# A dense f32r product on TensorE: operand addresses on multiples of 2048 bytes, and moving columns read and written backwards

## The reference: what is computed

```python
# first layer
p = rmsnorm(x, g) @ w_in                    # 1024 x 3076: r, k, v, decay, gates, q, kv, index
y = concat([y_rwkv, y_attn]) @ w_out        # 1024 x 1024
x = rmsnorm(x + y, final_g)
# second layer, mixer: 1024 x 9216, memory of 256 tokens: 1024 x 2048
proj = rmsnorm(x) @ w_in_2
k, vm = split(rmsnorm(mem) @ w_kv_2)
y_a = (gb * conv3(gc * v)) @ w_a_out        # 1024 x 1024
y_b = silu(layernorm(conv31(u * sigmoid(ug)))) @ w_b_out
y_c = attention(q, k, vm) @ w_att_out
x = x + (g0 * y_a + g1 * y_b + g2 * y_c) @ w_o
# second layer, feed-forward: 1024 x 5632, 2816 x 1024
gt, up = split(conv3(rmsnorm(x) @ w_up))
x = x + (silu(gt) * up) @ w_down
out = rmsnorm(x, norm_final_g)
```

## Time and profile before

| | |
|---|---|
| median of 3 runs | 1462.99 us |
| lowest, highest | 1462.32, 1467.27 us |
| span of the profiled execution | 1458.8 us |
| PE busy | 1410.6 us (97%), 7612 matmul records |
| PE weight loads busy | 1142.5 us (78%) |
| VectorE busy | 928.9 us (64%) |
| ScalarE busy | 495.1 us (34%) |
| GpSimdE busy | 493.1 us (34%) |
| mean granted TensorE clock | 0.983 of full speed |

### The profile page before, as it was taken

The page is one execution under the profiler, slowest core; times in us unless marked ns, Lnnn a source line. Parts: engine busy times, 40 slices in busy tenths (PEclk is TensorE's granted clock), DMA queues, the critical chain, the costliest instruction groups (busy, mean ns, idle before and its releaser), DMA issues.

```text
span 1458.8 us, 18647 instructions
## 1 busy us (share of the span) xinstructions
PE 1410.6 (97%) x7612; PEld 1142.5 (78%) x7612; DVE 928.9 (64%) x1327; ACT 495.1 (34%) x679; POOL 493.1 (34%) x139
## 2 busy tenths in 40 slices
PE   7999988899998999999999999999998999999998
PEld 6778646678797877888888887878886888888886
DVE  6679977435414355869969974761458888884122
ACT  5443476344324332222222223322234333332121
POOL 0004120113535322344344343334433333433441
PEclk9999999899999999999999999999999999999998
DMA  6221000203323212222322322222222222232221
GB/s 207 87 87 58 30 2 1 87 32 116 116 87 118 85 58 87 87 87 87 116 87 90 113 87 87 86 88 87 93 82 87 87 102 100 87 110 85 89 92 58
DMA packets 21349, 125.14 MB, mean 86 GB/s; under 512 B 2384, under 2 KB 3408, under 8 KB 7696
## 3 DMA queue, kind: packets, MB, share of 16 engines
q1 hardware_dynamic: 20752, 121.71, 23.6%
q10 hardware_dynamic: 512, 2.23, 0.4%
HBM read 121.84 MB, written 2.10 MB: 85 GB/s over the span
## 4 chain that ended last, share of the span: by engine, by line
PE 84%; DVE 11%; ACT 3%; issue 2%; DMA 0%; DVEq 0%; SPq 0%; ACTq 0%
PE bank L410 24%; PE bank L412 23%; PE bank L411 23%; DVE score L1988 2%; DVE misc L1987 2%; PE bank L361 1%; PE bank L1028 1%; PE bank L1044 1%; DVE conv_b L2489 1%; ACT prob L1463 1%; PE bank L679 1%; PE bank L401 1%; PE bank L896 1%; PE bank L977 1%; PE bank L634 0%
## 5 line engine op out<-in xcount | busy, mean ns | idle before, releaser
L1239 POOL TENSOR_TENSOR w_lo<-w_raw,w_hi 128x2048 fp32r<-128x2048 f32 (+1 forms) x102 | 468.6, 4594 | 755.2 <-ACT w_hi L1303 739.2
L410 PE MATMUL bank<-op_hi,w_hi 128*128 128x512 f32 x1312 | 517.2, 394 | 9.3 <-issue 6.5
L412 PE MATMUL bank<-op_hi,w_lo 128*128 128x512 f32 x1312 | 513.4, 391 | 0.0
L411 PE MATMUL bank<-op_lo,w_hi 128*128 128x512 f32 x1312 | 513.0, 391 | 0.0
L410 PEld LDWEIGHTS bank<-op_hi,w_hi 128*128 128x128 f32 x1312 | 247.3, 188 | 65.7 <-issue 9.7
L1303 ACT ACTIVATE w_hi<-w_raw 128x2048 fp32r<-128x2048 f32 (+2 forms) x109 | 205.7, 1887 | 269.2 <-PE bank L412 269.2
L411 PEld LDWEIGHTS bank<-op_lo,w_hi 128*128 128x128 f32 x1312 | 247.4, 189 | 52.9 <-issue 0.7
L412 PEld LDWEIGHTS bank<-op_hi,w_lo 128*128 128x128 f32 x1312 | 247.0, 188 | 53.1
L2382 DVE SCALAR_TENSOR_TENSOR bank<-pad_b,par,bank 128x512 f32<-128x512 f32 x232 | 175.3, 756 | 7.8
L2279 DVE TENSOR_TENSOR x_res<-bank,x_res 128x512 f32<-128x512 f32 x24 | 16.5, 691 | 132.8 <-PE bank L412 132.8
L2559 DVE TENSOR_TENSOR tmp<-tmp,conv_f 128x512 f32<-128x512 f32 x22 | 88.5, 4022 | 13.3 <-ACT tmp L1759 13.3
(11 more groups left out here) (394 smaller groups left out, 1782.4 us busy)
## 6 DMA issues: line engine op xcount, KB each, us to landing
w_raw<-in_w_units SPq DMA_DIRECT2D x104, 1024.0 KB, 4.8
w_raw<-in_w_units SPq DMA_DIRECT2D x4, 768.0 KB, 4.1
x_res<-in_x SPq DMA_DIRECT2D x8, 256.0 KB, 6.3
x_res<-in_x ACTq DMA_DIRECT2D x2, 1024.0 KB, 6.5
out<-x_res SPq DMA_DIRECT2D x8, 256.0 KB, 2.2
w_raw<-in_w_units SPq DMA_DIRECT2D x3, 512.0 KB, 8.2
w_raw<-in_w_units SPq DMA_DIRECT2D x4, 256.0 KB, 5.6
mem_tok<-in_mem SPq DMA_DIRECT2D x1, 1024.0 KB, 5.0
```

The source lines that it names most:

```text
L410: nc.tensor.matmul(b[:, 0:width], h, xh[:, x0 + k, 0:width], start=start and k == ks[0], stop=False)
L411: nc.tensor.matmul(b[:, 0:width], h, xl(x0 + k, width), start=False, stop=False)
L412: mm = nc.tensor.matmul(b[:, 0:width], l, xh[:, x0 + k, 0:width], start=False, stop=stop and k == ks[-1])
L1239: nc.gpsimd.tensor_tensor(w_lo[u % 2][:, 0:nk, :], w_raw[u % 2][:, 0:nk, :], w_hi[u % 2][:, 0:nk, :].bitcast(F32), ALU.subtract).then_inc( ...
```

## The change

Three things, in four places:

Then every moving tile of a dense product begins on a multiple of 2048, each chunk k of 512 columns fills exactly one such row, and the 128x128 weights begin on a multiple of 512.
- **Direction of reading.** In `tile` the moving operand is read from its last column to its first (step -1).
- **Direction of writing.** The bank is written from its last column to its first, so that each column lands where it did.

All other instructions keep their direction, those of L958 to L960 and the float32 matmuls among them. The number and order of instructions on every engine is the same as before.

```diff
+ROW = 2048
...
-        base = -(-nc.sbuf_base // 32) * 32
+        base = -(-nc.sbuf_base // ROW) * ROW
...
-        R0 = 133504
+        R0 = 66 * ROW
...
                     h, l = wh[:, k, col:col + P], wl[:, k, col:col + P]
-                    nc.tensor.matmul(b[:, 0:width], h, xh[:, x0 + k, 0:width], start=start and k == ks[0], stop=False)
-                    nc.tensor.matmul(b[:, 0:width], h, xl(x0 + k, width), start=False, stop=False)
-                    mm = nc.tensor.matmul(b[:, 0:width], l, xh[:, x0 + k, 0:width], start=False,
-                                          stop=stop and k == ks[-1])
+                    o, m_hi, m_lo = b[:, width - 1::-1], xh[:, x0 + k, width - 1::-1], xl(x0 + k, width)[:, width - 1::-1]
+                    nc.tensor.matmul(o, h, m_hi, start=start and k == ks[0], stop=False)
+                    nc.tensor.matmul(o, h, m_lo, start=False, stop=False)
+                    mm = nc.tensor.matmul(o, l, m_hi, start=False, stop=stop and k == ks[-1])
...
-    nc = bacc.Bacc("TRN2", target_bir_lowering=False, num_devices=1)
+    nc = bacc.Bacc("TRN2", target_bir_lowering=False, num_devices=1, dynamic_dma_scratch_size=1024)
```

## The result

The changed kernel takes 1487.6 us (median of 4 runs, 1477.7 to 1489.7), the kernel before 1464.2 in the same comparison: ratio 1.0141, 95% interval 1.0118 to 1.0165, or 23.4 us more. The profiled execution spans 1486.4 us; its own time was 1488.1, so 1.7 us lie outside the span.

A forecast was written before the change was run, and what follows sets the result against it. PE's dense 512-column matmuls were taken to bound the kernel through a surcharge; a gross gain of 66.7 us less 10.4 off the path left 56.3, and 1458.8 - 56.3 + 4.2 gave forecast 1407 us, range 1390 to 1467.

The forecast's parts named there:

- What bounds the kernel: PE bounds the kernel; its dense 512-column matmuls start 226.7 ns apart, 12.0 ns above the pace without surcharge.
- the forecast's floor of 214.7: Dense matmul on PE with no surcharge left: 214.7 ns, half of the float32 record's 0.429 us.
- placement and direction on PE, together: Dense matmuls on PE: no surcharge left, 214.7 ns, taken as likeliest; otherwise unchanged, 233.3 everywhere, or half feed at 0.427 us.
- The terms of the sum: Gross gains on PE: `op_*` 40.3 us; `op2_*`, `merged_*`, `raw_*` 16.5; `act_*` 8.6; `plain_*` 1.3; together 66.7.
- The discount of 10.4 us: Part of PE's gain not on the path, in four stretches where other engines bound: 3.1, 3.3, 2.5 and 1.5 us.
- Term (b): From 903.63 to 955.67, beside the layer norm: about 216 matmuls' gain, 3.3 us, returns as longer wait for `op_lo`.
- Term (c): Before 1125.67, where PE waits for GpSimdE's weight split: about 190 matmuls' gain, 2.5 us, is taken by that wait.
- Outside the span: Median 1463.0 against a profiled span of 1458.8: 4.2 us lie outside the span and stay.
- The first: Only placement counts, direction doesn't: shifted tiles come down to 226.7 ns, 8.3 us gained, 1455 us; chance 0.20 with what lies between.
- The second: Nothing changes, the surcharge being the plain cost of weights read beside columns: 1463 us; chance 0.08.
- The third: Starting on a multiple of 512 is itself bad: `op_*` goes to 233.3 ns, 22.2 us more, 1485 us; chance 0.09.
- The fourth: Columns read or written backwards are fed at half pace: 969 us more, about 2430 us; chance 0.11.

The follow-up runs named there:

- the other: Every moving tile and weight put 128 bytes past a multiple of 2048, read forward, against the kernel with the place alone: 1456.1 us, ratio 0.9954.
- the map: Synthetic kernel, no part of the reference: 39 streams of 96 dense f32r matmuls at different moving and weight starts; forward 226.7 to 238.0 ns per matmul.

## Why the prediction was wrong

**What bounds the kernel** was read rightly: the distance of the dense matmuls moved, and the waits by little. The surcharge that shows only at full feed is real: bf16, columns of step 0 and columns read twice all have 215.8 ns, and the float32 record has 0.429 us. Against 215.8 it is 10.9 ns; the forecast's floor of 214.7 was 1 ns too low. (The 119 ns for 256 columns are 118.3 by the earlier trace rows, 0.71 us for six; no term of the sum rests on it.)

**The step that failed** is "placement and direction on PE, together", where the prediction took 214.7 between bounds of 214.7 and 233.3, and the sentence behind it: that two streams read in the same direction would keep out of each other's way. Read backwards, a matmul takes 233.3 ns at distance 0, and no distance tried is better. Of the place, the prediction had seen that `op_*` and the weights already had the same remainder; forward at that distance 226.7 is the lowest that any stream had, so for 3360 of the 4872 matmuls the place had nothing left to give. The reason "half the feed makes it vanish, so the two streams have room beside each other" took a gain by half the rate as evidence for a gain by direction. It showed that half the feed makes room, not that backwards reading finds any at the full one.

The terms of the sum, as measured: `op_*` 3360 x +6.6 ns = +22.2 us where -40.3 stood; `op2_*`, `merged_*`, `raw_*` 0 instead of -16.5; `act_*` 528 x +2.4 = +1.3 instead of -8.6; `plain_*` about +0.4 instead of -1.3. Sum +23.9, against 23.4 between the medians. That the two meet so closely is luck: one kernel's executions differ by more, the changed kernel's by 12.0 us, and the mean granted clock with them (0.986 in the fastest of the four, 0.979 to 0.982 in the others). For the kernel with the direction alone the same sum gives 26.1 us (22.2 for `op_*`, 768 x 3.2 ns = 2.5 for `op2_*` and `merged_*`, 528 x 2.7 = 1.4 for `act_*`, which has 428 in 100 us there), where its median is 20.8 above that of the kernel before.

The discount of 10.4 us for what is off the path was worked out for a faster PE; with a slower one the waits for others should shrink instead. Term (b) is borne out: 216 matmuls at 6.6 ns are 1.4 us, and the wait fell by 1.2, from 1.66 to 0.44. Term (c) isn't: 190 matmuls make 1.3 us, and the wait before the split's unit fell by only 0.29, from 4.88 to 4.59. The split began later too (1141.80 against 1120.65, while the matmul behind it started at 1146.80 against 1125.67), so it moved along with PE instead of standing still. In the kernel with the place alone the wait of (b) grew to 2.4 us (PE's waits in the kernel with the place alone: who waited for whom, us in total, times, longest):

```profile
PE bank L411 <- DVE op_lo L1815: 2.4, 1, 2.4
```

**Outside the span** the prediction put 4.2 us; every execution whose time and span are both known has 1.7 to 1.9. The rest was the distance of one execution from the median. In the same way the profiled span of the kernel with the place alone (1458.4 us) hides its gain: it is the longest of its six (1452.6 to 1458.4), while the 1458.8 of the kernel before is shorter than every other span of that kernel that is known (1459.1 to 1466.1). Executions also differ by where the half clock falls: from 283 to 300, a stretch of small matmuls in the scan, the granted clock is 0.90 before and 0.60 in the kernel with the place alone. The window of the kernel before, then that of the kernel with the place alone:

```profile
283.00:300.00 17.00, 17.00 (x202) 14.94 (x201) 6.69 (x12) 8.91 (x16) 0.00 (x0) 0.90 0.50 187
```

and

```profile
283.00:300.00 17.00, 16.93 (x140) 14.49 (x141) 6.39 (x10) 4.18 (x9) 0.00 (x0) 0.60 0.49 187
```

**The rivals.** The first (only placement counts, 8.3 us) is what the place alone does: 6.1 us in one kernel, 7.2 in the other. What spoke against it in the prediction, that `op_*` lay at the weights' remainder and still paid 12 ns, was no argument: 226.7 is the lowest that any forward stream had here with a new f32r column each time. The second (nothing changes) is out. The third gave 1485 us and every tile at 233.3; time and pace came true, but by another mechanism, since the same places read forward have 226.7. That its numbers fit is luck; its chance was 0.09. The fourth (half pace) is out: a step of -1 costs 6.6 ns, while a step of 2 does double the time. The range, 1390 to 1467, left out both slower rivals, though the trace of forward reads offered no evidence at all on direction; a range that took in the third would have held the time.

**The pages.** The Trainium skill, "SBUF — State Buffer", section "SBUF: two separate sides", says that TensorE's reads wait for nobody. Here its pace moved from 226.7 to 233.3 ns with the moving tile's distance from the weights, so the measurement decides against what the prediction took from it, that placement couldn't matter. Whether TensorE waits for another reader or only for its own two streams isn't shown. The Trainium skill, "Advanced Engine Details and Errata", section "PSUM Cachelines", says that two consecutive elements should be contiguous. Writing the bank backwards alone had 226.8 ns, as forward: the trace agrees, if a step of -1 counts as contiguous, and the strict reading that the prediction gave to rival 4 is out.

**What stays open.** The surcharge needs a new four-byte moving column per column computed, and weights' addresses shift it; but it doesn't shrink with fewer weight columns (231.6 at 32), which speaks against a plain collision with each weight read. A stream of f32r matmuls without any weight load wasn't tried, since each such matmul brings its own. Why reading backwards loses the fast distances isn't settled either, nor why `act_*` forward had 230.9 ns, although most of it lies at a distance that has 232.4 to 233.4 in the map.

## What to carry to other kernels

Give moving operand and weights the same remainder (here modulo 256 bytes, both on multiples of 32) and read forward: in this kernel that is worth 0.5%, with the change's other half left out. Before an edit rests on how two streams meet, run the stream by itself: a single synthetic kernel of 96-matmul streams prices many places and directions at once, and nothing in a trace of forward reads speaks of backward ones. A rival whose time fits isn't thereby right; undoing each half of the change told the two apart.

## What the runs showed of the hardware

- A dense f32r stream of 512 new columns had 226.7 ns per matmul at best, bf16 215.8. The difference is gone when each moving column is read twice.
- Its pace hangs on the distance between moving start and weights' start, with a period of 256 bytes as far as tried: 226.7 to 227.2 at 0, 226.7 at 240 (one start tried), 230.0 at 48, 229.1 at 64, 232.4 to 234.3 at 32 and 96 and from 128 to 224.
- Reading 512 moving columns with step -1 has 233.3 to 236.6 ns in f32r at all eleven distances: 6.6 more than forward at distance 0, nothing more where forward has 233.3 already. In bf16 and float32 it costs nothing. Writing the bank with step -1 costs nothing. A moving step of 2 doubles the time (453 ns).
- Moving starts 4 or 16 bytes behind the weights' have 238.0 and 231.7 ns; both 16 past a multiple of 32 have 231.1.
